# Unread products on TensorE during the router's waits, and a reordered choice of experts

## What is computed

```python
h = h + merged @ w_out
u2 = rmsnorm(h, norm_ffn)                       # 512 x 1024
p_group = softmax(u2 @ wg + bg)                 # 4 groups, the best one is taken
e_logits = (u2 @ we + be)[best group]           # 8 experts per group
e_val, e_idx = top_k(softmax(e_logits), 2)      # two experts per token
for each expert: y += weight * (silu(u2 @ w_gate) * (u2 @ w_up)) @ w_down
out = rmsnorm(h + y, norm_final)
```

## Time and profile before

| | us |
|---|---|
| median of 3 runs | 1137.32 |
| lowest, highest | 1136.3, 1138.05 |
| the profiled execution, its own time | 1138.34 |
| its span | 1136.5 |

### The profile page before, as it was taken

One profiled execution on the slowest core, in us unless ns is written; L12 is line 12 of the kernel. 1 busy time (PEld: TensorE's weight loads), 2 busy tenths in 40 slices (PEclk: granted clock), 3 DMA queues, 4 the chain that ended last, 5 costly groups with the idle time before them and its releaser, 6 DMA issues.

```text
span 1136.5 us, 15499 instructions
## 1 busy us (share of the span) xinstructions
PE 1040.1 (92%) x6445; PEld 630.8 (55%) x6445; DVE 476.9 (42%) x972; ACT 314.8 (28%) x602; POOL 59.0 (5%) x69
## 2 busy tenths in 40 slices
PE   6999999998999999999999999999996999787780
PEld 6665656675575575575566566444454655344440
DVE  4536364637337337337335454523235321111115
ACT  3535344434234334334332122110110111100112
POOL 1000000000000000000000000000001222211110
PEclk9999999999999999999999999999996999988995
DMA  9322222233132132132112111044936999999945
GB/s 287 90 64 66 57 57 56 56 80 73 39 63 72 38 65 70 39 65 70 38 37 75 56 56 57 1 160 165 366 143 240 408 414 416 416 418 414 418 200 231
DMA packets 111946, 174.41 MB, mean 153 GB/s; under 512 B 9012, under 2 KB 87101, under 8 KB 103555
## 3 DMA queue, kind: packets, MB, share of 16 engines
q1 hardware_dynamic: 97890, 130.73, 33.3%
q10 hardware_dynamic: 8256, 31.53, 7.0%
q0 software_dynamic: 5728, 11.14, 3.9%
HBM read 169.16 MB, written 12.60 MB: 160 GB/s over the span
## 4 chain that ended last, share of the span: by engine, by line
PE 68%; DMA 14%; DVE 12%; ACT 3%; issue 2%; SPq 1%; POOL 0%; DVEq 0%; POOLq 0%
PE ps L746 21%; DMA arena<-in_expert_w_up 11%; PE ps L737 7%; PE ps L743 7%; PE ps L744 6%; PE ps L2001 6%; DVE arena L1284 4%; PE ps L1707 3%; PE ps L791 3%; PE ps L2008 2%; PE ps L770 1%; DVE arena L1441 1%; DVE yT L2330 1%; DVE arena L1520 1%; DVE arena L1517 1%
## 5 line engine op out<-in xcount | busy, mean ns | idle before, releaser
L746 PE MATMUL ps<-arena 128*128 128x512 f32 x672 | 314.0, 602 | 0.0
L746 PEld LDWEIGHTS ps<-arena 128*128 128x128 f32 x672 | 119.6, 190 | 113.6 <-issue 108.5
L2001 PE MATMUL ps<-arena,gates 128*64 128x256 f32 x864 | 107.7, 406 | 25.9 <-DMA arena<-in_expert_w_up 24.4
L743 PE MATMUL ps<-arena 128*128 128x264 f32 x416 | 127.9, 389 | 0.8 <-DVE gates L1356 0.8
L744 PE MATMUL ps<-arena 128*128 128x264 f32 x416 | 126.6, 386 | 0.0
L1284 DVE TENSOR_TENSOR arena<-arena 128x256 f32<-128x256 f32 (+6 forms) x194 | 91.5, 516 | 56.5 <-ACT arena L1105 34.3
L2001 PEld LDWEIGHTS ps<-arena,gates 128*64 128x64 f32 x864 | 65.0, 147 | 75.4 <-DMA arena<-in_expert_w_up 35.0
L737 PE MATMUL ps<-yT,arena 128*128 128x512 f32 x192 | 84.8, 596 | 2.2 <-DVE gates L1356 1.4
L744 PEld LDWEIGHTS ps<-arena 128*128 128x128 f32 x416 | 79.0, 190 | 13.5
L743 PEld LDWEIGHTS ps<-arena 128*128 128x128 f32 x416 | 76.0, 190 | 16.3 <-issue 4.7
L2156 DVE COPY gates<-ps 128x1024 f32<-128x1024 f32 x16 | 19.6, 1225 | 110.7 <-PE ps L1988 110.7
(11 more groups left out here) (329 smaller groups left out, 1257.8 us busy)
## 6 DMA issues: line engine op xcount, KB each, us to landing
arena<-in_w_in SPq DMA_DIRECT2D x68, 512.0 KB, 3.8
arena<-in_expert_w_gate SPq DMA_DIRECT2D x27, 1024.0 KB, 28.9
arena<-in_expert_w_up SPq DMA_DIRECT2D x27, 1024.0 KB, 34.6
arena<-in_expert_w_down ACTq DMA_DIRECT2D x18, 1024.0 KB, 32.7
arena<-in_w_branch SPq DMA_DIRECT2D x12, 512.0 KB, 3.9
C<-in_expert_w_gate SPq DMA_DIRECT2D x5, 1024.0 KB, 32.3
gates<-in_expert_w_up SPq DMA_DIRECT2D x5, 1024.0 KB, 38.5
arena<-in_w_out SPq DMA_DIRECT2D x1, 4096.0 KB, 13.8
```

Source lines behind the costliest of these rows:

```text
L743: t.matmul(dst[:, 0:HALF], wt, uT[:, k, 0:HALF], start=(k == 0), stop=(k == KD - 1))
L746: mm = t.matmul(dst, wt, uT[:, k, META:], start=(k == 0), stop=(k == KD - 1))
L2001: mm = t.matmul(dst, toks[:, k, :], src, start=(k == 0), stop=(k == KD - 1))
```

## The change

TensorE gets `keep_busy(n)`: n products of the identity (128x128) with 512 columns of the transposed rows into PSUM bank 5, which nobody reads. It runs 15 of them between the router's last product and the wait for `M`, 2 between the counts and the table, and 11 behind the table, ahead of the wait for the first fetched pair. The logits of the last tile get a PSUM bank of their own, bank 1. VectorE scales and biases the first three tiles (`sc`, `lb`) before it copies the last half tile, waiting for a new step `l2` of TensorE, and the last tile in one operation (`l3`). The last tile's `normed` (`u3`) moves from behind `num` to ahead of `l3`; its store on ScalarE's queue moves ahead of `eg` and `e2`. The group mask `og` is made twice as long (both choices), `o1` and `o2` become halves of `o12`, and `O1`, `O2` one operation `O`. `dm` moves behind `num`. The same is computed.

```diff
             pe2 = Steps(..., ["o0", ..., "o7", "l2", "T3b", "lg", "rk", "ct", "tb"])
-            choose = ["sc", "lb", "gm", "lt", "gd", "gx", "og", "el", "es", "m1", "e1", "q1", "x1", "o1",
-                      "n2", "m2", "e2", "q2", "x2", "o2", "dm", "O1", "O2", "M", "num", f"u{NT - 1}"]
+            choose = ["l3", "gm", "lt", "gd", "gx", "og", "el", "es", "m1", "e1", "q1", "x1", "o1",
+                      "n2", "m2", "e2", "q2", "x2", "o2", "O", "M", "num", "dm"]
-            rows_order = [..., "u2", "t3a", "h7", "t3b"]
+            rows_order = [..., "u2", "t3a", "h7", "sc", "lb", "t3b", "u3"]
...
+                a.wait_ge(*dve2.after(f"u{NT - 1}"))
+                a.dma_start(u2_dram[(NT - 1) * P:, :], u2[:, NT - 1, :]).then_inc(sem("rows_kept"), 16)
                 a.wait_ge(*dve2.after("lt"))
                 a.activation(gx, lt, ACT.Exp).then_inc(*act2.did("eg"))
                 a.wait_ge(*dve2.after("dm"))
                 a.activation(e2, dm, ACT.Exp).then_inc(*act2.did("e2"))
-                a.wait_ge(*dve2.after(f"u{NT - 1}"))
-                a.dma_start(u2_dram[(NT - 1) * P:, :], u2[:, NT - 1, :]).then_inc(sem("rows_kept"), 16)
+
+            def logit_bank(i):
+
+                return bank(0)[:, i * 36:(i + 1) * 36] if i < NT - 1 else bank(1, 36)
...
-                        mm = t.matmul(bank(0)[:, i * 36:(i + 1) * 36], u2T[:, k, i * P:(i + 1) * P], wr[:, k, :],
+                        mm = t.matmul(logit_bank(i), u2T[:, k, i * P:(i + 1) * P], wr[:, k, :],
...
+                def keep_busy(n):
+
+                    for _ in range(n):
+                        t.matmul(bank(5), ident, u2T[:, KD - 1, :], start=True, stop=True)
...
-                logits(2, every, "t2")
+                logits(2, every, "t2").then_inc(*pe2.did("l2"))
                 turn_tokens(3, high_half, "T3b")
                 logits(3, low_half, "t3a")
                 logits(3, high_half, "t3b").then_inc(*pe2.did("lg"))
 
+                keep_busy(15)
                 t.wait_ge(*dve2.after("M"))
...
                 mm.then_inc(*pe2.did("ct"))
+                keep_busy(2)
...
                 mm.then_inc(*pe2.did("tb"))
+                keep_busy(11)
...
+                step, tt, ts, red, slots_of = small_steps(v)
+                first = NT - 1
+                v.wait_ge(*pe2.after("l2"))
+                tt("sc", lg[:, 0:first, :], bank(0, first * 36).rearrange("p (i c) -> p i c", i=first),
+                   ss2[:, 0:first].unsqueeze(2).broadcast_to([P, first, 36]), ALU.mult)
+                tt("lb", lg[:, 0:first, :], lg[:, 0:first, :], over(rb, first), ALU.add)
                 turned(NT - 1, 1)
+                normed(NT - 1)
...
                 v.wait_ge(*pe2.after("lg"))
-                v.wait_ge(*act2.after(f"rs{NT - 1}"))
-                tt("sc", lg, bank(0, NT * 36).rearrange("p (i c) -> p i c", i=NT), ss2.unsqueeze(2).broadcast_to([P, NT, 36]), ALU.mult)
-                tt("lb", lg, lg, over(rb, NT), ALU.add)
+                step("l3", v.scalar_tensor_tensor(lg[:, first, :], logit_bank(first), ss2[:, first:NT], rb, ALU.mult, ALU.add))
...
-                tt("dm", dm, m2, m1, ALU.subtract)
-                for k, o_ in ((0, o1), (1, o2)):
-                    tt(f"O{k + 1}", chosen[:, k, :].rearrange("p (i g e) -> p i g e", i=NT, g=NG),
-                       og.unsqueeze(3).broadcast_to([P, NT, NG, NE]), o_.unsqueeze(2).broadcast_to([P, NT, NG, NE]), ALU.mult)
+                tt("O", chosen.rearrange("p k (i g e) -> p (k i) g e", i=NT, g=NG), og.unsqueeze(3).broadcast_to([P, 2 * NT, NG, NE]),
+                   o12.unsqueeze(2).broadcast_to([P, 2 * NT, NG, NE]), ALU.mult)
                 tt("M", mm_, chosen[:, 0, :], chosen[:, 1, :], ALU.add)
                 tt("num", numbered, by_expert, NUM.unsqueeze(2).broadcast_to([P, 2 * NT, NX]), ALU.mult)
-                normed(NT - 1)
+                tt("dm", dm, m2, m1, ALU.subtract)
```

## The result

| | median us | runs | lowest to highest |
|---|---|---|---|
| before | 1137.26 | 4 | 1136.3 to 1138.05 |
| changed | 1147.72 | 4 | 1143.93 to 1150.39 |

The ratio of the executions is 1.0082, 95% interval 1.0065 to 1.0100 (the two medians give 1.0092): slower, by 10.5 us between the medians. A second series beside the kernel before gave 1144.15 us against 1137.95, ratio 1.0060 (1.0047 to 1.0072), 6.2 us. The forecast was 1145.7 us, 1142 to 1149. The profiled execution of the changed kernel took 1143.93 us, the lowest of its four; its span is 1142.0 us, its mean granted clock 0.986 where it was 0.970. The other three have 0.984 (1145.96 us), 0.981 (1150.39 us) and 0.974 (1149.49 us) and no trace.

A forecast was written before the change was run, and what follows sets the result against it. Behind the routing, full DMA engines bound the kernel, so the weight stream's start sets the end. `pair_turned(0)` moves +6.8 - 1.0 + 4.35 - 0.8 = +9.35 us, less 0.9 is 8.4; 1137.32 + 8.4 = 1145.7 us, range 1142 to 1149.

The forecast's parts named there:

- The price of a product: In all three waits on TensorE: one unread product is two records, 0.858 us at full clock; 15, 2, 11 take 12.87, 1.72, 9.44.
- The list of signs: Expected in the trace after: 30, 4, 22 records at 0.43 us, rank at 863, turning near 876, DMA idle until 878 us.
- Hidden VectorE work: First wait: VectorE's reordering, worth 0.7 to 0.8 us with few products, is hidden under the 15 products.
- The stream's start: Behind the routing: the weight stream becomes continuous 8.4 us later, bounds 7.25 and 9.35, and the end moves by this.
- the sag: Transfers between `pair_turned(0)` and `up_made(0)`: the 1.1 us dip to 89 GB/s closes, worth 0.9 us.
- Rival (a): First wait: the clock falls anyway, costing 1.7 to 2.2 us more, 1147.4 to 1147.9 us; chance 0.29.
- Rival (b): All three waits: an unread product takes one record of 0.43 us, not two, so the change is faster, 1133.8 us; chance 0.09.
- Rival (c): Experts' stage: loads with spare time absorb PE's late start, 1137 to 1138.5 us, chance 0.05; half absorbed 1141 to 1143, 0.07.

The follow-up runs named there:

- 0, 0 and 11 products: Changed kernel with no unread products in the first two waits and 11 in the third: 1141.08 us, ratio 1.0034 to the kernel before.
- 6, 0 and 5: Changed kernel with 6, 0 and 5 unread products in the three waits instead of 15, 2 and 11: 1132.75 us, again 1134.33; ratios 0.9954, 0.9966 to before.
- earlier loads: Changed kernel with 6, 0 and 5 products, last two first weight loads (2 MB) not waiting for `pair_turned(0)`: 1137.50 us, ratio 0.9999 to before.

## Why the prediction was right, and where it was off

**The price of a product** held: 56 records, 0.43 us each. Forecast against measured, the measured ones 0.3 us late from the start: rank 862.97, 863.28; `M` about 855.4, 855.8; rank start to table end 4.45, 4.65 us; the last 11 9.44, 9.54 us; `pair_turned(0)` 878.1, 878.5; `up_made(0)` 883.25, 883.7. The list of signs has the turning near 876 us, but the prediction's own sum puts its start at 876.9; it came at 877.47.

**Hidden VectorE work** held: the products on the kernel before move `up_made(0)` as far as in the changed one, and the reordering without products starts the rank 0.7 us sooner, the 0.7 to 0.8 of the prediction.

**The stream's start** is the term that was mis-sized. I took `pair_turned(0)` less 0.9 us for the sag, 8.4 us, and named 7.25 from `up_made(0)` as a bound. The last `up` started 6.9 us later, in the second series 6.9 too. The experiments say which is nearer: in all kernels that leave the loads in place the last `up` moves as `up_made(0)` does, within 1.3 us (-6.1 us for -5.6, +7.2 for +7.9, +20.0 for +20.7). The medians say the same: but for the changed kernel's first series, each differs from the one beside it by what `up_made(0)` moved, within 1.1 us. `pair_turned(0)` does not fit so well. With 0, 0 and 11 products its release, the first of these rows, came 5.1 us later than before, with 6, 0 and 5, the second row, 3.4 us sooner:

```profile
873.94 0.33 SPq L1953 DMA_DIRECT2D gates<-in_expert_w_up  x1
```

```profile
865.38 0.33 SPq L1953 DMA_DIRECT2D gates<-in_expert_w_up  x1
```

Less 0.9 these would be +4.2 and -4.3 us; the medians moved by +3.1 and -5.5, `up_made(0)` by +3.0 and -5.6. So a full set of transfer engines behind that stage was right, and the time at which it starts was the bound and not the value: the closed sag was worth 2.9 us and not 0.9 in the changed kernel (9.8 - 6.9), 2.6 in these two. In the prediction's own sum its main term is 1.1 us too much.

Why the sag was worth that much is not shown. A count of bytes speaks for the prediction's value: at `up_made(0)` the changed kernel had moved about 1.4 of the 2.1 MB released (880.00 to 883.70 us at 369 GB/s and a little before), the kernel before nearly all. The 0.7 MB left, an estimate of 1.6 us at 414 GB/s, do not appear in the start of the last `up`. Moving all 2 MB behind `up_made(0)` costs 5 us all the same, and moving them ahead of `pair_turned(0)` brought about 1 us beside `up_made(0)` (-3.0 for -1.8).

**The end of the kernel** has a term that the prediction did not have: the last `up` stands behind a wait of 2 us for its weights and runs at half clock in some executions (5.18 to 5.36 us) and not in others (3.67). That is 1.5 to 1.7 us in the traces of different kernels; no kernel but the changed one and 6, 0 and 5 was traced twice, and in those it was 3.67 each time. Between the traces of before and after it hid a part of the loss.

**Rival (a)**, the clock falling among the first products, did not happen in the profiled executions with 15 or 30 products (1.00 in the row of 850.64 to 863.28 us). It can happen all the same: it came in one of the four traced executions with 6 in the first wait, the one with earlier loads, for 3.4 us, and made the products 1.7 us longer, the lower of the two prices given. How often is not known. **Rival (b)**, cheap products, fell on the 30 records. What is left of it shows with 6, 0 and 5: products that end inside the wait cost nothing, and the change then gains what the warm clock gives. **Rival (c)** fell with 30 products.

The Trainium skill's advice, "TensorE: Matmul & The Clock Gate", section "Why this matters for your kernels", to leave no idle gaps of some microseconds between bursts, agrees with the runs in part. In the changed kernel, with products in all three waits, the clock stayed at 1.00. Wherever the first wait was empty it fell in it, and with 6 or 15 in the first and none in the third it fell in the third. But the fall in the kernel before came 0.6 us after PE's last product, when the gap was no longer than that, and with the earlier loads it fell while the products ran (0.50 from 850.70, 0.51 from 860.90 us). The advice says nothing of what the filling costs where it is longer than the gap, and that was the result: the sum of all waits that went was 11 us, the products that took their place 24 us.

What stays open: why the changed kernel's medians were 10.5 and 6.2 us above in two series, with 7.7 for the products alone. The forecast of 8.4 lies between them. By `up_made(0)` its main term is 1.1 us too large, so the measured 1147.72 us should lie below the forecast and lies above it: the first series has a loss that the sum does not have, and the nearness of the two numbers is in part luck.

## What to carry to other kernels

Unread work that keeps a clock up must end before the wait that it fills is over; count it in the trace's records, since one f32 product is two of them, and size it by the wait that is left once the clock is up. Behind the stage, ask which release makes the stream of transfers continuous, and forecast that time; what was only moved around ahead of it brought little here.

## What was not expected of the hardware

A group of products started at half clock still paid: ten records took 6.32 us instead of 4.56, but `up_made(0)` came 2.0 us sooner than without them, because the clock rose among them and not in `up(0)`. And behind six products in the first wait the clock stayed up over the thin rank and table products (rank to table's end 3.6 us, 5.5 before), in all four traced executions with six, but not over the 5 us of idle time that follow where the third wait is empty.
